# When a weight slot counts as free, and what stands ahead of the first norm, in a streaming encoder step on one core

## What is computed

```
c_act = silu(c)
for l in range(2):
    shift_m, scale_m, gate_m, shift_f, scale_f, gate_f = split(c_act @ w_ada[l] + b_ada[l], 6)
    h = rmsnorm(x, g_norm_mix[l]) * (1 + scale_m) + shift_m
    x = x + gate_m * token_mixer(h, w_in[l], ..., w_branch[l], w_out[l])
    h = rmsnorm(x, g_norm_ffn[l]) * (1 + scale_f) + shift_f
    x = x + gate_f * (swiglu(h) if l == 0 else moe_swiglu(h, w_router, b_router, ...))
y = rmsnorm(x, g_final)
```

## Time and profile before

| what | value |
|---|---|
| median of 3 runs | 1528.15 us (1525.77 to 1528.89) |
| time of the profiled execution | 1528.08 us |
| its span, first to last instruction | 1526.3 us |
| TensorE busy | 1414.5 us (93%) |
| VectorE, ScalarE, GpSimd busy | 1024.2, 783.3, 40.3 us |
| mean granted TensorE clock | 0.958 of full |
| read from memory | 310.84 MB |

### The profile page before, as it was taken

How to read it: one execution, slowest core, us unless ns; L and a number is a source line. 1 busy time by engine, 2 the same in 40 slices (tenths; PEclk the granted TensorE clock), 3 DMA queues, 4 the chain that set the end, 5 groups by cost and what they waited for, 6 DMA issues and landing times.

```text
span 1526.3 us, 24618 instructions
## 1 busy us (share of the span) xinstructions
PE 1414.5 (93%) x9375; PEld 1253.1 (82%) x9375; DVE 1024.2 (67%) x1417; ACT 783.3 (51%) x1059; POOL 40.3 (3%) x66
## 2 busy tenths in 40 slices
PE   5899999998889999998999999987999999999984
PEld 4788998875889999997999988766788888888863
DVE  1476998775454444425879886644588988889855
ACT  1534447634433333225444675243477887878752
POOL 0000100000000000000001000000200000000100
PEclk8899999999989999999999999998699999999996
DMA  9856743124446877435767651246389999999952
GB/s 288 216 178 200 236 141 121 60 83 152 141 132 200 247 228 240 163 89 146 228 195 254 209 151 53 96 134 227 116 309 384 384 383 388 378 386 385 383 208 67
DMA packets 280084, 327.33 MB, mean 214 GB/s; under 512 B 32304, under 2 KB 190456, under 8 KB 279992
## 3 DMA queue, kind: packets, MB, share of 16 engines
q1 hardware_dynamic: 273042, 314.29, 62.0%
q10 hardware_dynamic: 5478, 6.53, 1.2%
q0 software_dynamic: 1472, 5.24, 1.0%
HBM read 310.84 MB, written 15.17 MB: 214 GB/s over the span
## 4 chain that ended last, share of the span: by engine, by line
PE 88%; DVE 5%; ACT 2%; DMA 2%; issue 2%; ACTq 1%; SPq 0%; POOLq 0%; DVEq 0%; POOL 0%
PE mmp L804 14%; PE mmp L806 13%; PE mmp L805 13%; PE mmp L1202 8%; PE mmp L1204 8%; PE mmp L1203 8%; PE mmp L798 7%; PE px L854 2%; PE py L774 2%; PE py L870 2%; PE px L774 1%; PE lg L969 1%; PE lg L774 1%; PE px L1011 1%; DVE hT L1772 1%
## 5 line engine op out<-in xcount | busy, mean ns | idle before, releaser
L804 PE MATMUL mmp<-hT_hi,wm_hi 128*128 128x320 f32 (+1 forms) x976 | 308.4, 316 | 11.1 <-issue 5.8
L806 PE MATMUL mmp<-hT_hi,ring_lo 128*128 128x320 f32 (+1 forms) x976 | 306.1, 314 | 0.0
L805 PE MATMUL mmp<-hT_lo,wm_hi 128*128 128x320 f32 (+1 forms) x848 | 263.9, 311 | 0.0
L1803 DVE TENSOR_TENSOR ring_lo<-ring,wm_hi 128x1024 fp32r<-128x1024 f32 (+1 forms) x124 | 148.2, 1201 | 93.1 <-ACT wm_hi L1408 90.7
L804 PEld LDWEIGHTS mmp<-hT_hi,wm_hi 128*128 128x128 f32 (+1 forms) x976 | 184.8, 189 | 16.5 <-issue 8.9
L806 PEld LDWEIGHTS mmp<-hT_hi,ring_lo 128*128 128x128 f32 (+1 forms) x976 | 184.6, 189 | 0.2
L1408 ACT CAST wm_hi<-ring 128x1024 fp32r<-128x1024 f32 (+1 forms) x124 | 126.6, 1028 | 96.9 <-PE mmp L806 78.4
L805 PEld LDWEIGHTS mmp<-hT_lo,wm_hi 128*128 128x128 f32 (+1 forms) x848 | 160.1, 189 | 0.1
L1363 ACT ACTIVATE tmp<-mmp 128x320 f32<-128x320 f32 x70 | 30.6, 438 | 233.8 <-PE mmp L806 164.7
L1891 DVE SCALAR_TENSOR_TENSOR conv<-u_conf,dwc,conv 128x350 f32<-128x350 f32 x240 | 132.2, 582 | 3.1
L804 PE MATMUL mmp<-h_hi,wd_hi 128*128 128x320 f32 x352 | 111.3, 316 | 8.8 <-DVE h_lo L2050 8.8
(11 more groups left out here) (364 smaller groups left out, 2893.8 us busy)
## 6 DMA issues: line engine op xcount, KB each, us to landing
ring<-in_w_in_dram SPq DMA_DIRECT2D x104, 512.0 KB, 4.5
ring<-in_w_exp_in_dram SPq DMA_DIRECT2D x64, 512.0 KB, 8.1
more<-in_w_exp_in_dram SPq DMA_DIRECT2D x64, 512.0 KB, 11.3
ring<-in_w_ada_dram SPq DMA_DIRECT2D x56, 512.0 KB, 6.9
more<-in_w_exp_out_dram SPq DMA_DIRECT2D x48, 512.0 KB, 5.5
ring<-in_w_ffn_in_dram SPq DMA_DIRECT2D x44, 512.0 KB, 5.9
wide<-in_w_ada_dram SPq DMA_DIRECT2D x40, 512.0 KB, 7.5
ring<-in_w_branch_dram SPq DMA_DIRECT2D x48, 256.0 KB, 2.8
```

Of the source, the lines that this page charges most:

```text
L804: nc.tensor.matmul(out, w_hi, x_hi, start=is_first, stop=False)
L805: nc.tensor.matmul(out, w_hi, x_lo, start=False, stop=False)
L806: return nc.tensor.matmul(out, w_lo, x_hi, start=False, stop=is_last)
L1803: V.tensor_tensor(mix_rows(ring_lo, l, s, r), mix_rows(ring, l, s, r), mix_hi(l, s, r).bitcast(F32), ALU.subtract).then_inc(mix_lo_ready, 1)
```

## The change

Four things are done.

1. The semaphores `slot_free` go. SyncE waits on the count of the engine that reads the slot last: TensorE's `chunk_done`, or for the feed-forward's chunks VectorE's `lo_ready`. ScalarE no longer raises a semaphore for each chunk, and VectorE no longer waits for its own subtraction to raise one.
2. TensorE does modulation pairs 0 and 1 ahead of the norm's sums. Pairs 2 and 3 follow, each after the transpose of the pair two before it.
3. ScalarE copies pairs 0 and 1 out ahead of the norm's root.
4. `row_loads(1)` and the two router transfers are issued by ScalarE after the casts of split chunk 1 (`mix_high(1, 1)`) of layer 0.

```diff
@@ block.sync
-            def load(n, parts, it=None, fills=1):
-
-                if it is not None:
-                    sp.wait_ge(slot_free[n % SLOTS], it * fills + n // SLOTS)
-                elif n >= SLOTS:
-                    sp.wait_ge(slot_free[n % SLOTS], n // SLOTS)
+            split_from = {ring_no["ffn", 0, k]: k for k in range(NFFN)}
+
+            def slot_wait(n):
+
+                if n in split_from:
+                    sp.wait_ge(lo_ready, split_from[n] + 1)
+                elif n >= 0:
+                    sp.wait_ge(chunk_done, n + 1)
+
+            def load(n, parts):
+
+                slot_wait(n - SLOTS)
...
-                            sp.wait_ge(slot_free[k], (n0 - 1 - k) // SLOTS + 1)
+                            slot_wait(n0 - SLOTS + (k - n0) % SLOTS)
@@ block.tensor
             ada_pair(0, 0)
+            ada_pair(0, 1)
             norm_sums(0)
-            for m in range(1, ADA_FIRST):
-                ada_pair(0, m)
-                ada_turn(0, m - 1)
-            ada_turn(0, ADA_FIRST - 1)
+            for m in range(ADA_FIRST):
+                ada_turn(0, m)
+                if m + 2 < ADA_FIRST:
+                    ada_pair(0, m + 2)
@@ block.scalar
-            def chunk_wait(n, split=False):
+            def chunk_wait(n):
 
                 act.wait_ge(chunk_done, n + 1)
-                if not split:
-                    act.sem_inc(slot_free[n % SLOTS], 1)
...
                     ada_evac(0, 0)
+                    ada_evac(0, 1)
                     norm_std(0)
-                    row_loads(1)
-                    act.dma_start(wr[:], w_router[0].rearrange("(c p) e -> p c e", p=P)).then_inc(router_loaded, 16)
-                    act.dma_start(br[:], b_router[0:1, :]).then_inc(router_loaded, 16)
-                    for m in range(1, ADA_FIRST):
+                    for m in range(2, ADA_FIRST):
                         ada_evac(0, m)
...
                 for r in range(2):
                     mix_high(1, r)
+                if l == 0:
+                    row_loads(1)
+                    act.dma_start(wr[:], w_router[0].rearrange("(c p) e -> p c e", p=P)).then_inc(router_loaded, 16)
+                    act.dma_start(br[:], b_router[0:1, :]).then_inc(router_loaded, 16)
@@ block.vector, low(k)
                                     wd_hi[:, k % 2, 0:size].bitcast(F32), ALU.subtract).then_inc(lo_ready, 1)
-                    dve.wait_ge(lo_ready, k + 1)
-                    dve.sem_inc(slot_free[n % SLOTS], 1)
```

More of the change, by code:

```diff
@@ L377, in build @@
         chunk_done = sem("chunk_done")
-        slot_free = [sem(f"slot_free{i}") for i in range(SLOTS)]
         hi_ready = sem("hi_ready")
@@ L1356, in pair, with to_tmp @@
                 return mmp[0:m, 2 * (pair_no[stage, l, j] % 2) + b, 0:T]
-            def to_tmp(stage, l, j, f0, f1, t, split=False):
-                chunk_wait(ring_no[stage, l, j], split)
+            def to_tmp(stage, l, j, f0, f1, t):
+                chunk_wait(ring_no[stage, l, j])
                 if t >= 2:
@@ L1600, in _ @@
                         if k < FC:
-                            to_tmp("ffn", l, k, ACT.Silu, ACT.Copy, tmp_before["ffn_in", l] + k, split=True)
+                            to_tmp("ffn", l, k, ACT.Silu, ACT.Copy, tmp_before["ffn_in", l] + k)
                         if k + 2 < NFFN:
```

## The result

| | median | runs | ratio to before |
|---|---|---|---|
| before | 1528.46 us | 1525.71 to 1529.91 (6) | |
| after | 1518.85 us | 1515.09 to 1521.63 (6) | 0.9933 [0.9916, 0.9951] |

The kernel is faster by 0.67%, 9.6 us, where 5.8 had been forecast.

The account below looks back on a forecast made before the run. TensorE, 88% of the chain, was taken as the bound, so freeing slots pays only where it waits for transfers, in the opening. 1528.1 - 5.5 (opening) - 0.3 (raises and waits) = 1522.3 us, range 1519.9 to 1526.8.

Parts of the forecast that it names:

- The opening: Stretch up to the first projection: with slots freed earlier and pair 1 ahead of the sums, projection at 35.5, 5.5 us earlier.
- the bounds 30.2 to 32.0: Landing of chunk 7 in the opening: 30.2 at the fast transfer rate, 32.0 if chunk 8 interleaves; 30.9 taken.
- So I take the second half at the full level: Second half of modulation pair 3, after chunk 7 lands: 1.07 us at 2.4 GHz instead of 1.98, 0.9 us saved.
- The clock of the projections: First projections: low clock, 0.63 over 7.35 us, left unchanged; 1.0 us more gain if it held, chance 0.10.
- The clock falls in the opening: Rival, chance 0.07: TensorE, idle 1.6 us before chunk 3, drops its clock; projection at 40.2, total 1527.0, no change.
- interleaving: Rival, chance 0.14: transfers of chunks 8 and 9 slow chunk 7's past 32.0; projection at 38.3, total 1525.1.
- Hidden. Counted: 0: Row and router transfers moved behind split chunk 1: issues of 4.4 us fit ScalarE's idle time, chunk 14's delay costs TensorE nothing.
- the bound of 3.5: Delay of chunk 14 by the moved row and router transfers: at most 3.5 us, at least nothing, 1 taken.
- The room of 3.5 us: At split chunk 2: slack before TensorE needs chunk 14's low part, as large as the delay's whole upper bound.
- ScalarE's issues were not held up: Rival, chance 0.06: the 13 moved issues throttled behind saturated transfers; gain gone from 1.2 us each, 1531.5 at 1.5.
- Between 0 and 1.0 I take 0.3: Gain behind the opening from raises and waits removed on ScalarE and VectorE: 0.3 us.
- the bound of 1.0: Upper end for removed raises and waits: 0.6 us on ScalarE, at 0.17 us per raise, and 0.4 on VectorE.

Follow-up runs that it names:

- raise_rest: After, with ScalarE's raise, which nobody waits for, put back for every chunk that had one before, but not for the gates; 1514.70 us, one run.
- raise_gates: After, with ScalarE again raising a semaphore, which nobody waits for, between wait and first sigmoid for the 24 gate chunks; 1523.08 us.
- late_raise: Before, with ScalarE raising the slot's semaphore behind its two sigmoids, not ahead of them, for the 24 gate chunks; 1521.02 us.
- the idle Silu: A one-column silu per layer that nobody reads, added behind the layer norm's root; on after 1514.70 and 1512.08 us, on before 1528.81 us.
- silu_before: Before, with only a one-column silu per layer that nobody reads added behind the layer norm's root; 1528.81 us, ratio 0.9996.

## Why the prediction was right or wrong

**The opening: right in size, by luck.** Forecast 5.5 us at the first projection and the same behind it; measured 4.05 at the projection (36.93 against 40.98) and 5.63 at the cache transposes. What was lost ahead of the projection the clock gave back behind it, and other traces with the same opening reach the transposes 1.4 us earlier to 2.3 us later than after's.
- Chunk 7 landed at 31.4, forecast 30.9, within the bounds 30.2 to 32.0.
- "So I take the second half at the full level" failed: 1.93 us, not 1.07. The mean of 0.93 over 5.09 us makes (0.93 - 0.5) / 0.5 x 5.09 = 4.4 us at the full level, so the clock fell at 31.0, just ahead of that half. TensorE had by then stood idle for 1.46 us, done the first half in 1.08 and stood idle again from 29.8; what before's trace had shown, a fall 2.8 us into one long idle stretch, did not carry over. From landing to projection it took 5.51 us as before (5.54), not 4.6.
- The clock of the projections, left as it was, rose from 0.63 to 0.71 (10.99 us for 32 matmuls, not 11.57), and split chunk 0 ran at full clock where it had run at half for 6 us. From split chunk 0 to the cache transposes it is 1.1 us shorter in spite of the 1.47 us wait.
- *The clock falls in the opening* and *interleaving* did not come: the clock is 1.00 from 20.93 to 26.61, and chunk 7 landed before 32.

**The moved rows: "Hidden. Counted: 0" was wrong by the 1.47 us in after's trace.** The delay of chunk 14, taken as 1 us, is some 1.3 by the landings told above, well inside the bound of 3.5. The room of 3.5 us was reckoned with chunk 14's landing in old times plus 1 us and with one copy out. In after the split chunks come 4.5 us earlier but chunk 14 only 2.9 (65.64 against 68.58), and a copy and a table load of 1.28 us stand between cast and free bank. That uses the room up where split chunk 0 runs at the full clock, and not where it runs at half. ScalarE's issues were not held up: 0.3 to 0.5 us each, as in the earlier trace rows.

**The failed step: "Between 0 and 1.0 I take 0.3".** The term for raises and waits that go measured 9.1 us: 8.17 in the gates, 0.34 in the branches, 0.58 at the feed-forward. The bound priced a raise by its own duration. As a sum over all raises that was right: 0.34 us in the branches (`raise_rest`) and 0.58 at the feed-forward, 0.92 against the bound of 1.0; the 0.17 us that the prediction took for one raise is here what all raises of a layer's branches cost together. `raise_gates` and `late_raise` show what the bound left out, 8.17 us: the instruction that the raise keeps behind the wait. The rows were there to be read: ScalarE's 18 table loads at L1453 each carried a wait for TensorE, 1.28 us that no data called for. I had read only casts and copies on ScalarE. The Trainium skill ("ScalarE: Activation LUTs", section "Table sets: the hidden batching unit") advises to batch activations by table set, which would price a load by its count. Here the count stays at 18 and 8.2 us go: where the load stands decides. The same page of the Trainium skill (section "What ACT_TABLE_LOAD costs") adds a drain of about 1.38 us to the 1.28 of the load; in this trace the activation starts within 0.02 us of the load's end (67.03 + 1.28, 68.32), and the load within 0.01 of the copy ahead of it, so a switch of tables costs 1.28 us here and not 2.66.

**What held the total near the forecast.** Opening and removed raises make 5.63 + 9.1 = 14.7 us; the clock took 5.9 back, of it 5.22 from conf to expert, with the same work there. Over 13 traces that stretch is 124.4 to 124.6 us (four), 126.6 (two) or 128.8 to 130.8 (seven), in kernels with and without each edit, and its mean granted clock is 0.85, 0.82 and 0.79 to 0.81. So in the traces the clock accounts for the gap between 14.7 and the span's 8.9 us. That it also explains why medians of -9.5 and -5.1 us make -9.6 is possible but not shown; which edit brings about which level there was not found, and it may be none. The claim that the idle Silu is worth 5.8 us holds roughly for after (3.5 and 6.8 measured) and not for before (none), and this too is left open. Why the conf matmuls keep the full clock in `raise_gates`, whose idle time ahead of them is after's, was not settled either.

## What to carry to other kernels

In all thirteen traces an ACT_TABLE_LOAD of the gates ran ahead of its activation's wait where nothing stood between wait and activation, and behind it where a raise did: raise a semaphore behind the activation, not ahead of it, or load the table earlier with an activation that nobody reads. In a timeline look at which of the two rows carries the bracket: a load with a wait in it is up to 1.28 us to be had, where the chain runs through it. Here nine loads per layer had one, and three waits of TensorE on the chain came from them. And price a removed instruction by what it kept waiting behind it, not by its own duration.

## What the runs showed of the hardware that was not expected

- A lone semaphore raise on ScalarE is nearly free (0.17 us per layer for those of the branches), yet put between a wait and an activation it costs 1.36 us at each place on the chain: 102.14 us with it, 98.05 to 98.06 without, in the traces of before, after and seven of the experiments; with the idle Silu the stretch is 98.2 or 102.3.
- 1.28 us less idle time of TensorE went with more than itself: behind 1.7 to 1.8 us idle the 48 matmuls took 13.17 us in eight stages of eight, behind 3.0 to 3.1 us idle 14.6 to 16.2 us in fourteen of eighteen, and 13.17 in four.
- The same kernel, or the same work in different kernels, comes out at different clock levels: `silu_before` took 1520.3 to 1520.7 us in three runs and 1528.0 to 1530.7 in eight, and a stretch of the same work 124.4 to 130.8 us over 13 traces.
